# Where the modulation tiles stand in the list of loads of a two-block float32 kernel: two turns further back

## The reference, cut to what matters

```python
# first block
shift, scale, gate = split(silu(c) @ w_ada + b_ada, 3)          # w_ada: 2048 x 6144
h = rmsnorm(x) * (1 + scale) + shift
p = h @ w_in                                                   # q, k, v, z_a, u_b, z_b, g_a, g_b
y = (g_a * ((attn * silu(z_a)) @ w_pa) + g_b * ((fourier * silu(z_b)) @ w_pb)) @ w_out
x = rmsnorm(x + gate * y)
# second block
shift1, scale1, gate1, shift2, scale2, gate2 = split(silu(c2) @ w_mod + b_mod, 6)   # w_mod: 2048 x 12288
u = rms(x) * (1 + scale1) + shift1
proj = u @ w_in2          # stick-breaking attention, gated delta rule, gates
h = x + gate1 * (merged @ w_out2)
u = rms(h) * (1 + scale2) + shift2
h = h + gate2 * ((silu(u @ w_gate) * (u @ w_up)) @ w_down)
```

## Time and profile before

| | us |
|---|---|
| time, median of 3 runs (lowest, highest) | 2800.46 (2799.1, 2802.19) |
| the profiled execution's own time | 2796.57 |
| its span | 2794.7 |
| TensorE busy (matmul) | 2759.4 |
| VectorE busy | 2048.6 |
| ScalarE busy | 1460.1 |
| POOL busy | 379.5 |

### The profile page before, as it was taken

How to read it: one execution, slowest core, us unless ns; L and a number is a source line. 1 busy time by engine, 2 the same in 40 slices (tenths; PEclk the granted TensorE clock), 3 DMA queues, 4 the chain that set the end, 5 groups by cost and what they waited for, 6 DMA issues and landing times.

```text
span 2794.7 us, 42931 instructions
## 1 busy us (share of the span) xinstructions
PE 2759.4 (99%) x16354; PEld 2384.1 (85%) x16354; DVE 2048.6 (73%) x3589; ACT 1460.1 (52%) x2414; POOL 379.5 (14%) x958
## 2 busy tenths in 40 slices
PE   7999999999999999999999999999999999999999
PEld 4778888888888888888888888888888888888888
DVE  4468878888987788888888877778976555555554
ACT  3465544445566666666666444545454443344443
POOL 0014300000002344434343320000000000000000
PEclk9999999999999999999999999999999999999999
DMA  9946668888955455555555678888856555555564
GB/s 359 349 160 217 221 216 284 294 304 307 308 167 203 163 176 177 180 172 177 176 182 178 219 235 271 295 290 286 276 179 225 185 186 190 192 186 193 183 198 142
DMA packets 183582, 621.84 MB, mean 223 GB/s; under 512 B 20288, under 2 KB 28752, under 8 KB 182736
## 3 DMA queue, kind: packets, MB, share of 16 engines
q1 hardware_dynamic: 173360, 605.62, 63.8%
q10 hardware_dynamic: 10016, 13.47, 1.5%
HBM read 612.70 MB, written 4.21 MB: 221 GB/s over the span
## 4 chain that ended last, share of the span: by engine, by line
PE 82%; DVE 7%; ACT 4%; POOL 3%; DMA 2%; issue 2%; ACTq 0%; SPq 0%; DVEq 0%
PE ps L96 81%; DVE wlo L111 2%; POOL small L111 2%; DMA raw<-in_w 1%; POOL small L114 1%; DVE acc L117 1%; PE ps L99 1%; ACT whi L102 1%; DVE c_y L117 1%; ACT sb_l L102 1%; DMA raw<-in_w_s 0%; ACT L105 0%; DMA xc<-in_xc 0%; ACT sb_z L102 0%; DMA q_sw<-q_g 0%
## 5 line engine op out<-in xcount | busy, mean ns | idle before, releaser
L96 PE MATMUL ps<-act,whi 128*128 128x512 f32 (+1 forms) x6560 | 1657.8, 392 | 6.8 <-DVE p_x L111 5.8
L96 PEld LDWEIGHTS ps<-act,whi 128*128 128x128 f32 (+1 forms) x6560 | 1176.0, 188 | 224.0 <-issue 8.0
L111 DVE TENSOR_TENSOR wlo<-raw,whi 128x1024 fp32r<-128x1024 f32 (+3 forms) x883 | 1039.2, 1186 | 19.5 <-ACT whi L102 15.1
L102 ACT ACTIVATE whi<-raw 128x1024 fp32r<-128x1024 f32 (+3 forms) x883 | 897.1, 1028 | 260.2 <-PE ps L96 103.0
L96 PE MATMUL ps<-act,wlo 128*128 128x256 f32 (+2 forms) x6416 | 972.3, 290 | 0.0
L96 PEld LDWEIGHTS ps<-act,wlo 128*128 128x128 f32 (+1 forms) x6416 | 868.7, 190 | 56.2 <-issue 9.2
L117 DVE SCALAR_TENSOR_TENSOR acc<-raw,c_act,acc 128x1024 f32<-128x1024 f32 x210 | 268.3, 1278 | 0.0
L114 POOL TENSOR_SCALAR small<-small 128x2 f32<-128x2 f32 (+3 forms) x316 | 138.7, 439 | 950.1 <-DVE small L114 820.2
L111 POOL TENSOR_TENSOR small<-small 128x2 f32<-128x2 f32 (+1 forms) x460 | 166.5, 362 | 345.0 <-ACT u_u L102 310.8
L111 DVE TENSOR_TENSOR w_u<-w_u,ps 128x256 f32<-128x256 f32 x44 | 18.4, 421 | 99.3 <-ACT w_u L102 99.3
L111 DVE TENSOR_TENSOR w_g<-w_g,ps 128x256 f32<-128x256 f32 x44 | 18.4, 421 | 93.4 <-ACT w_g L102 93.4
(11 more groups left out here) (328 smaller groups left out, 2299.7 us busy)
## 6 DMA issues: line engine op xcount, KB each, us to landing
raw<-in_w SPq DMA_DIRECT2D x418, 512.0 KB, 4.7
raw<-in_w_mod SPq DMA_DIRECT2D x192, 512.0 KB, 5.3
raw<-in_w_gate SPq DMA_DIRECT2D x88, 512.0 KB, 4.4
raw<-in_w_up SPq DMA_DIRECT2D x88, 512.0 KB, 4.1
raw<-in_w_s SPq DMA_DIRECT2D x64, 512.0 KB, 6.9
raw<-in_w_out SPq DMA_DIRECT2D x64, 512.0 KB, 5.8
raw<-in_w_down SPq DMA_DIRECT2D x64, 448.0 KB, 4.4
raw<-in_w_ada SPq DMA_DIRECT2D x32, 512.0 KB, 5.0
```

What stands on the lines that cost most here:

```text
L96: return self.e.matmul(*args, **more)
L102: return self.e.activation(*args, **more)
L111: return self.e.tensor_tensor(*args)
```

## The change

In the list of loads the modulation tile of turn K stood right behind the weights of turn K. It now stands right behind the weights of turn K+2. Nothing else differs: VectorE reads it at the same place of its own order, the seven buffers and the wait on the load seven places before stay, and only the buffer number of many loads changes with their place.

```diff
@@ -496,8 +496,8 @@
     n_start = len(LOADS)
     for turn in TURNS:
         w_raw[turn.t] = load(turn.source, turn.cols, ("lo", 16 + turn.t), turn.shape)
-        for k, m in enumerate(plan.mods.get(turn.t, ())):
-            m_raw[turn.t, k] = load(m[4], 1024, ("m", *m[:1], *m[2:4]))
+        for k, m in enumerate(plan.mods.get(turn.t - 2, ())):
+            m_raw[turn.t - 2, k] = load(m[4], 1024, ("m", *m[:1], *m[2:4]))
     raw = lambda r: RAW[r % NR]
     landed = lambda r: on("landed", r)
```

## The result

The changed kernel takes 2806.56 us (median of 16 runs, 2801.78 to 2812.15), the kernel before 2799.81 us (16 runs, 2795.82 to 2803.95). The ratio is **1.0022**, with a 95% interval of 1.0014 to 1.0029: +6.7 us by the medians, in the range and close to the forecast of +5. The profiled execution has a span of 2804.6 us against 2794.7, which is 9.9 us.

A forecast was written before the change was run, and what follows sets the result against it. TensorE, busy 99% of the span, was taken as the bound. Merge-stage late tiles (+3 us) and weights (+2 us) gave +5 us on the 2800.46 us median: 2805.5 us, range 2796.5 to 2819.

The forecast's parts named there:

- Three steps between release and reading: Merge stage: each modulation tile's slot is released three VectorE steps ahead of its reading, five before, in all 59 tiles.
- the wait of VectorE for the tiles: A new VectorE wait for modulation tile loads, 20 to 50 us in all, nearly all from 430 to 690 us.
- no change past 700 us: All stretches past 700 us were to keep their lengths within 1 us.
- The periods: Merge stage: the time of one output tile n, seven turns, forecast at 17.2 to 18.5 us.
- SP's waits for acc: SP's waits for modulation passes to free slots: to shrink to near nothing, while those for wlo grow.
- The gain side: Merge stage weight loads: costed at +2 us, three critical loads 0.95 us later, less what the others return.
- Rival (b): Landing stays below 5.3 us and weights come a little earlier: up to 6 us back, 2794.5 to 2797 us; chance 0.08.
- The loss side: Merge stage: modulation tiles land late and hold VectorE, making it slower by 3 us.
- the chain of 29 links of three steps: Steps 73 to 173: late tiles delay later releases; with 13 plain steps 255.4 us, against 252.35 before.
- The stages costed at nothing: Stages at 160 to 400, 860 to 1580 and 1800 to 2110 us: tiles nearly always in time, no cost.
- The bound of 5.0 us of landing: Merge stage: at 5.0 us landing the chain takes 229 us, never binds, and up to 6 us come back.
- The rule of the Trainium skill: About 2.0 us plus bytes over 436 GB/s, so about 3.2 us for 512 KB; by it no tile is late.

The follow-up runs named there:

- e2: Kernel before, with only the modulation tiles of turns 74 to 174 loaded two turns later: 2810.0 us, ratio 1.0032 to the kernel before.
- e3: Kernel before, with all modulation tiles except those of turns 74 to 174 loaded two turns later: 2797.85 us, ratio 0.9991 to the kernel before.
- e4: Changed kernel, but modulation passes read a resident tile and do not wait for the landing; SP waits instead: 2794.44 us, ratio 0.9977 to before.
- e8: Changed kernel, with VectorE's low pass put ahead of the modulation pass in each step: 2789.45 us, ratio 0.9959 to the kernel before.
- e1: Kernel before, with each modulation tile loaded one turn later instead of two: 2791.43 us, ratio 0.9968 to the kernel before.
- e5: Kernel before, but modulation passes read a resident tile and SP waits for the landing instead: 2800.0 us, ratio 0.9998 to before.
- e6: Kernel before, with each modulation tile loaded three turns later instead of two: 2910.37 us, ratio 1.0393 to the kernel before.

## Why the prediction held, and where a term was off

**The mechanism held: late modulation tiles in the merge stage.** Three steps between release and reading, the wait of VectorE for the tiles (20 to 50 us foreseen, 26.7 measured in the stage, 31 in all), the stage (255 to 262 us foreseen, 262.2 measured), p_x from 5.8 to 10.1 us, and no change past 700 us: each is in the profile after. The periods are 17.2 to 19.9 us, where 17.2 to 18.5 were foreseen. e2 and e3 show the place, e4 the cause. SP's waits for acc were to shrink to near nothing: the view of SP's waits has no row for them any more, all 2235 us of its main wait are for wlo.

```profile
SPq L129 <- DVE wlo L111: 2235.2, 860, 10.1
```

**The gain side was mis-sized, and in sign.** I put the weights at +2 us, from the recorded ends: three critical loads 0.95 us later. e4 measures -5.6 us. The step that failed is the reading of the recorded ends, and the choice of three loads out of it. Worked out again from the same trace, by a rule that gives each issue of before within 0.03 us, 93 weight loads from 460 to 690 us go out 1.0 us earlier in the mean (from 5.7 us earlier to 2.1 later), where the prediction has 0.05 us. Turns 113, 120 and 127 do move 0.9 us later, but those of 134 and 141 move 1.5 us earlier and not 0.3. e4 agrees: there a weight load goes out 6.3 us before ScalarE is free for it, in the mean of turns 75 to 175, against 5.6 us before. Rival (b) named up to 6 us back; that part of it was true, and the waits of VectorE buried it.

**The loss side was mis-sized as well: 3 us forecast, about 12 measured.** The prediction's distances do not come out of the trace either: the same rule gives a median of 5.7 us, 27 of 53 below 5.9 and 37 us of lateness, where it has 5.3, 32 and 47. And the chain of 29 links of three steps, of landings for two thirds of its length, is not what the profile after shows. The prediction took the median landing of before, 5.9 us, for every link. In the mean the modulation tiles of turns 74 to 174 landed faster in the changed kernel, 5.4 us against 5.8. With 5.4 the same sum gives 29 x 7.68 + 18.2 = 241 us, below the 252 of before: a chain of mean landings does not bind at all. What the chain of waits after has is a mixture, about one landing in each period: ten of modulation tiles and four of weights over the 14 periods, a third of its length, with the passes and joins of VectorE and TensorE's own work between them. The ten average 6.15 us, up to 7.75, more than the mean of all: the chain goes through the slow ones.

```profile
509.50 6.53 DMA raw<-in_w_mod
...
527.60 7.11 DMA raw<-in_w_mod
...
545.42 5.13 DMA raw<-in_w
...
676.08 7.75 DMA raw<-in_w_mod
```

The two errors, +2 for -5.6 and +3 for +12, nearly cancelled; that +5 came so close was luck. The stages costed at nothing were right: 4.4 us of VectorE's waits outside the merge stage moved none of the stretches between turns 20 and 866 by more than 1.1 us. The bound of 5.0 us of landing ("never binds, up to 6 us come back") came out in e8 and e1 at more than that, 10.6 and 8.6 us: the 6 us counted only the waits that TensorE shows. In e1 TensorE's idle time in the stage falls from 5.6 to 0.2 us, and its busy time for the same matmuls falls by 1.6 us as well.

The landings of modulation tiles in this stage, 5.4 us in the mean and up to 8.3 us at a DMA share of 0.86, with two to four other loads in flight at most issues, are what makes them late. The rule of the Trainium skill ("DMA: Bandwidth & Descriptors", anatomy of one DMA), fitted to DMAs of the gpsimd path, gives an estimate of about 3.2 us for 512 KB. By it next to no tile would have been late; for these loads, issued by SP, the trace does not agree with it.

**Open.** How the 12 us split between joins that stand behind the waiting pass and the releases behind it was not measured apart. e8 removed nearly all waits at once, so it does not tell what each us of wait costs, nor whether the distance or the opened link did it.

## What to carry to other kernels

In a ring of buffers that are filled in the order of a list, moving one kind of tile back brings every other kind forward: count both distances, from the release to the reading, in the shortest turns of the program, and compare them with the landing under load, its slow cases and not its mean. The best place is where both just fit; here it was one turn, neither none nor two. And the order inside an engine's step moves these distances too, one up and the other down: putting the low pass first was worth 17 us with one list and cost 13 us with the other, so try both orders with each list.

## What the runs showed of the hardware

A wait of TensorE can be followed by a stretch at half its clock, and then costs more than its length. In the trace after, TensorE waits 1.90 us for p_x before 571.41, and from 572.5 us on its granted clock is 0.5, the 1.2 GHz level, for 3.4 us. The sixteen matmuls from 571.41 on take 4.33 us, the sixteen from 575.74 on 2.86 us: about 1.5 us of the stage's growth. By stretch (columns of the earlier trace rows), 5 us each:

```profile
565.00:570.00 5.00, 4.52 (x28) 3.84 (x26) 3.61 (x5) 1.72 (x3) 0.00 (x0) 1.00 0.87 287
570.00:575.00 5.00, 3.59 (x13) 3.07 (x14) 1.80 (x3) 2.26 (x5) 0.00 (x0) 0.75 0.98 382
575.00:580.00 5.00, 5.00 (x28) 4.42 (x28) 4.80 (x7) 1.08 (x2) 0.00 (x0) 0.91 0.45 136
```

Not every such wait is followed by it. In e5 TensorE has a wait of the same length for the same join, and the clock stays up. The first eight matmuls behind it, in the trace after and in e5 (start, us):

```profile
571.41 2.82 PE L96 MATMUL ps<-act,whi 128*128 128x512 f32 x8 [1.90 <-DVE p_x L111]
...
567.10 2.09 PE L96 MATMUL ps<-act,whi 128*128 128x512 f32 x8 [1.90 <-DVE p_x L111]
```

The longest wait of the changed kernel in this stage, 2.74 us until 628.07, has no fall behind it either. What decides between the two is not shown.

In the kernel before the clock did not fall in this stage. In e2 it fell three times there, for 13.7 us together, and this can be why its profiled stage is 2.9 us above that of the full change: TensorE's idle time in the stage is the same in both (12.7 and 12.8 us), and its busy time is 3.0 us longer in e2. In e6 it was at 0.5 for 41 us of the merge stage, and TensorE's busy time there is 263 us against 247 before: some 16 of the 59 us that the stage grew are slower matmuls and not waits. Its mean is 0.94 over the stretch from 460 to 690 us:

```profile
460.00:690.00 230.00, 196.69 (x1038) 163.67 (x1036) 158.61 (x237) 89.21 (x147) 0.00 (x0) 0.94 0.75 242
```
